# First norm taken on the token rows and transposed a second time; early work of the last delta head put in another order

## What is computed

```python
h = rmsnorm(x, norm_w[0])                       # 320 x 2048
proj = h @ delta_w_in                           # q, k, v, z and 64 gate columns
... causal convolution, gated delta rule over 32 value heads ...
x = x + out @ delta_w_out                       # 4096 -> 2048
h = rmsnorm(x, norm_w[1])
... causal multi-scale pooling, gate, pool_w_out ...
x = x + out ; y = rmsnorm(x, final_norm_w)
```

## Time and profile before

| | |
|---|---|
| median of three runs | 2074.68 us (2072.94 to 2075.6) |
| the profiled execution, its own time | 2073.34 us |
| its span | 2071.6 us |
| TensorE busy (matmuls) | 2045.4 us, 99% of the span |
| DVE busy | 1261.4 us, 61% |
| ACT busy | 934.5 us, 45% |
| mean granted clock of TensorE | 0.993 |

### The profile page before, as it was taken

How to read it: one execution, slowest core, us unless ns; L and a number is a source line. 1 busy time by engine, 2 the same in 40 slices (tenths; PEclk the granted TensorE clock), 3 DMA queues, 4 the chain that set the end, 5 groups by cost and what they waited for, 6 DMA issues and landing times.

```text
span 2071.6 us, 51668 instructions
## 1 busy us (share of the span) xinstructions
PE 2045.4 (99%) x19451; PEld 1962.3 (95%) x19451; DVE 1261.4 (61%) x2245; ACT 934.5 (45%) x2013; POOL 155.3 (7%) x354
## 2 busy tenths in 40 slices
PE   8999999999999999999999999999999999999997
PEld 7999999999999999999899999999999999999997
DVE  5766677776667777667744445545546656644444
ACT  5555555555555556555533334333333333433333
POOL 4111011100101111010000010000000000000010
PEclk9999999999999999999999999999999999999999
DMA  6544555544455555445544445454454445444442
GB/s 208 163 137 127 162 152 163 152 137 132 138 163 153 153 151 146 123 139 164 162 152 157 140 145 178 143 163 144 152 167 147 150 141 164 158 156 148 143 157 77
DMA packets 381227, 311.13 MB, mean 150 GB/s; under 512 B 20041, under 2 KB 377114, under 8 KB 380570
## 3 DMA queue, kind: packets, MB, share of 16 engines
q1 hardware_dynamic: 379290, 306.30, 48.7%
q10 hardware_dynamic: 1872, 3.96, 0.6%
HBM read 283.85 MB, written 27.25 MB: 150 GB/s over the span
## 4 chain that ended last, share of the span: by engine, by line
PE 92%; DVE 6%; issue 1%; ACT 1%; DMA 0%; POOL 0%; DVEq 0%; ACTq 0%; POOLq 0%; SPq 0%
PE ps L298 27%; PE ps L299 26%; PE ps L300 26%; PE ps L1220 10%; DVE s_s L1153 2%; PE ps L1375 2%; DVE wlo L289 1%; DVE silu L1016 1%; DVE silu L1014 1%; DVE amat L1163 1%; PE ps L1346 0%; DVE xlo L893 0%; DVE xlo L1008 0%; DMA ht<-ht_save 0%; PE ps L1349 0%
## 5 line engine op out<-in xcount | busy, mean ns | idle before, releaser
L298 PE MATMUL ps<-xhi,whi 128*128 128x320 f32 x3072 | 984.8, 321 | 3.9 <-DVE wlo L289 2.6
L300 PE MATMUL ps<-xhi,wlo 128*128 128x320 f32 x3072 | 950.4, 309 | 0.0
L299 PE MATMUL ps<-xlo,whi 128*128 128x320 f32 x3072 | 950.2, 309 | 0.0
L289 DVE TENSOR_TENSOR wlo<-wraw,whi 128x1024 fp32r<-128x1024 f32 (+1 forms) x484 | 582.0, 1223 | 236.6 <-ACT whi L284 234.1
L284 ACT ACTIVATE whi<-wraw 128x1024 fp32r<-128x1024 f32 (+1 forms) x484 | 498.6, 1050 | 309.7 <-PE ps L300 278.6
L298 PEld LDWEIGHTS ps<-xhi,whi 128*128 128x128 f32 x3072 | 578.0, 188 | 28.4 <-issue 13.8
L299 PEld LDWEIGHTS ps<-xlo,whi 128*128 128x128 f32 x3072 | 578.7, 188 | 0.9
L300 PEld LDWEIGHTS ps<-xhi,wlo 128*128 128x128 f32 x3072 | 577.9, 188 | 0.0
L298 PE MATMUL ps<-bhi,whi 128*128 128x320 f32 x512 | 157.6, 308 | 0.0
L299 PE MATMUL ps<-blo,whi 128*128 128x320 f32 x512 | 157.6, 308 | 0.0
L300 PE MATMUL ps<-bhi,wlo 128*128 128x320 f32 x512 | 157.6, 308 | 0.0
(11 more groups left out here) (342 smaller groups left out, 2063.5 us busy)
## 6 DMA issues: line engine op xcount, KB each, us to landing
wraw<-in_delta_w_in_dram SPq DMA_DIRECT2D x384, 256.0 KB, 3.0
wraw<-in_pool_w_in_dram SPq DMA_DIRECT2D x256, 256.0 KB, 3.0
wraw<-in_delta_w_out_dram SPq DMA_DIRECT2D x128, 256.0 KB, 3.3
wraw<-in_pool_w_out_dram SPq DMA_DIRECT2D x128, 256.0 KB, 3.2
s_s<-in_state_delta_dram SPq DMA_DIRECT2D x32, 512.0 KB, 6.1
out_dram<-s_s SPq DMA_DIRECT2D x32, 512.0 KB, 4.2
wraw<-in_pool_w_group_dram SPq DMA_DIRECT2D x64, 256.0 KB, 3.1
dec<-gc_rows SPq DMA_DIRECT2D x16, 320.0 KB, 4.1
```

Of the source, the lines that this page charges most:

```text
L289: nc.vector.tensor_tensor(wlo[:, slot, 0:width], wraw[:, slot, 0:width], whi[:, slot, 0:width].bitcast(F32), ALU.subtract).then_inc(E("w_l ...
L298: mm(o, whi[:, slot, w], hi[:, k_x, :], start=first, stop=False)
L299: mm(o, whi[:, slot, w], lo[:, k_x, :], start=False, stop=False)
L300: done = mm(o, wlo[:, slot, w], hi[:, k_x, :], start=False, stop=last)
```

## The change

At the start, the scale by the reciprocal root is applied to the token rows (`x_rows`, in the memory of `branch`), by ACT for the first block of 128 tokens and by DVE for the other two, in two halves of 1024 channels. PE transposes these rows once more, tile after tile, in the same five banks. The weight goes into the two split operations, which read the transposed tile: ACT's copy to `xhi` takes it as a scale, DVE's to `xlo` is one multiply and subtract. `gates_tile(k - 5)` stands behind the transposes of tile k. The diagonal blocks, `rb`, the ring `sq` and the six matmuls on them go. Copies to `ht` are divided anew between ACT and DVE, DVE's first three stand ahead of the mean, and 24 small matmuls of the warm-up become 4.

In the last head, the quarters 1 to 3 of the branch split and the first two weight splits are spread over the head's first steps, and the two early jobs come two splits later.

```diff
-    BY_ACT = (0, 2, 4, 6) + tuple(range(8, KT))
-    BY_DVE = (1, 3, 5, 7)
+    BY_ACT = (3, 4, 6, 8, 10, 12, 14)
+    BY_DVE = (0, 1, 2, 5, 7, 9, 11, 13, 15)
...
     (ACT, start)
+        tile(3)
+        act.wait_ge(E("rinv"), 1)
+        for h in range(2):
+            c = slice(1024 * h, 1024 * h + 1024)
+            sc.activation(x_rows[:, c], xtok[:, 0, c], ACT.Copy, scale=small[:, 9:10]).then_inc(E("xs_act"), 1)
+        for k in BY_ACT[1:]:
             tile(k)
+        act.wait_ge(E("vecs"), 1)
         for k in range(KT):
+            if k % 4 == 0:
+                split_hi(act, k // 4, k // 4, 512)
+            act.wait_ge(E("xnorm"), k + 1)
+            sc.activation(xhi[:, k, :], tile_bank(k)[:, 0:T], ACT.Copy, scale=vecs[:, k:k + 1]).then_inc(E("x_hi"), 1)
...
     (ACT, delta)
-            begun()
-            split(0)
-            split(1)
+            if not quarter:
+                split(0)
+                split(1)
             decays(n)
             rounds(act, n)
             cached()
...
             last.then_inc(E("squares"), 1)
+            if quarter:
+                quarter(1)
             act.wait_ge(E("qkv_ps"), n * 3)
...
             last.then_inc(E("squares"), 1)
+            if quarter:
+                split(0)
+                quarter(2)
             act.wait_ge(E("z_evac"), n)
             sc.activation(gate[:], zraw[:], ACT.Tanh, scale=0.5).then_inc(E("z_tanh"), 1)
+            if quarter:
+                split(1)
+                quarter(3)
             split(2)
...
     (DVE, start)
-        tile(1)
+        for k in BY_DVE[0:3]:
+            tile(k)
         dve.wait_ge(E("sumsq"), 3)
...
+        for h in range(2):
+            for m, rows in ((1, P), (2, 64)):
+                v.tensor_scalar(x_rows[0:rows, DM * m + 1024 * h:DM * m + 1024 * h + 1024], xtok[0:rows, m, 1024 * h:1024 * h + 1024],
+                                small[0:rows, 9 + m:10 + m], None, ALU.mult).then_inc(E("xs_dve"), 1)
+        dve.wait_ge(E("vec_ps"), 1)
...
+        for k in BY_DVE[3:]:
+            tile(k)
...
+        for k in range(KT):
+            if k % 4 == 0:
+                split_lo(dve, k // 4, k // 4, 512)
             dve.wait_ge(E("x_hi"), k + 1)
+            v.scalar_tensor_tensor(xlo[:, k, :], tile_bank(k)[:, 0:T], vecs[:, k:k + 1], xhi[:, k, :].bitcast(F32),
+                                   ALU.mult, ALU.subtract).then_inc(E("x_lo"), 1)
...
     (DVE, early jobs)
-            if j in (3, 7):
-                early_job(j // 4)
+            if j in (5, 9):
+                early_job(j // 4 - 1)
...
     (PE, start)
-        for _ in range(24):
+        for _ in range(4):
             one(ps[0:BL, 3, 0:16], ident[0:BL, 0:BL], ident[0:BL, 0:16])
...
         for k in range(KT):
+            if k % 8 == 0:
+                pe.wait_ge(E("xs_act"), k // 8 + 1)
+                pe.wait_ge(E("xs_dve"), k // 4 + 2)
+            if k < 5:
+                tile_kept(pe, max(j for j in range(KT) if j % 5 == k))
+            else:
+                pe.wait_ge(E("x_lo"), k - 4)
+            b = tile_bank(k)
+            tr(b[:, 0:P], x_rows[:, P * k:P * k + P], ident[:])
+            tr(b[:, P:2 * P], x_rows[:, DM + P * k:DM + P * k + P], ident[:])
+            tr(b[:, 2 * P:T], x_rows[0:64, 2 * DM + P * k:2 * DM + P * k + P], ident[0:64, 0:64]).then_inc(E("xnorm"), 1)
+            if k >= 5:
+                gates_tile(k - 5)
+        for k in range(KT - 5, KT):
             gates_tile(k)
-        pe.wait_ge(E("rb"), 1)
+        pe.wait_ge(E("vecs"), 1)
```

More of the change, by code:

```diff
@@ L151, in build @@
     xtok = place(g, "xtok", [3, DM])
[L152 to L155, removed]
+    x_rows = branch[:, 0:20, :].rearrange("p k t -> p (k t)")
     vrow = place(g, "vrow", [P])
@@ L584, in delta_act @@
             act.wait_ge(E(f"x_in{m}"), 16)
-            sc.activation(sq_x[0:rows, DM * m:DM * m + DM], xtok[0:rows, m, :], ACT.Square,
+            sc.activation(x_rows[0:rows, DM * m:DM * m + DM], xtok[0:rows, m, :], ACT.Square,
                           accum_out=small[0:rows, 3 + m:4 + m]).then_inc(E("sumsq"), 1)
-        tile(0)
         act.wait_ge(E("ms"), 1)
@@ L712, in branch_hi, with delta @@
             sc.activation(xhi[:, 4 * ch:4 * ch + 4, :], branch[:, 4 * ch:4 * ch + 4, :], ACT.Copy).then_inc(E("b_hi"), 1)
-        def delta(n, split, cached, store, next_silus, begun, v_next, tail_next):
-            begun()
-            split(0)
-            split(1)
+        def delta(n, split, cached, store, next_silus, quarter, v_next, tail_next):
+            if not quarter:
+                split(0)
+                split(1)
             decays(n)
@@ L841, in out_split @@
             split_hi(act, OUT_A + LEAD + j, (LEAD + j) % 4)
-        def out_begun():
-            for ch in range(1, 4):
-                branch_hi(ch)
         act.wait_ge(E("w_used"), OUT_A)
         branch_hi(0)
-        delta(NH, out_split, lambda: None, lambda: None, lambda: None, out_begun, lambda: None, lambda: None)
+        delta(NH, out_split, lambda: None, lambda: None, lambda: None, branch_hi, lambda: None, lambda: None)
     def delta_dve(dve):
@@ L1017, in silus, with delta @@
                                    ).then_inc(E("silu"), 1)
[L1019 to L1023, removed]
+        def delta(n, d, split, conv_next, weights_next, decays_next, silus_next, quarter):
+            if not quarter:
+                split(0)
+                split(1)
             rounds(dve, n)
@@ L1252, in delta_pe @@
                     last = tr(ps[:, 2, P * h:P * h + P], crow[:, h, :], ident[:])
-            if k == 6:
-                pe.wait_ge(E("consts"), 8)
-                pe.wait_ge(E("diag"), 1)
-                for m, rows in enumerate((P, P, 64)):
-                    last = one(ps[:, 0, P * m:P * m + rows], ones[0:rows, :], diag[0:rows, P * m:P * m + rows])
-                last.then_inc(E("rb_ps"), 1)
-        for k in range(KT):
+                last.then_inc(E("vec_ps"), 1)
+        for k in range(KT):
+            if k % 8 == 0:
[12 more added lines that the diff above has]
+        for k in range(KT - 5, KT):
             gates_tile(k)
-        pe.wait_ge(E("rb"), 1)
+        pe.wait_ge(E("vecs"), 1)
         def project(i, at, count):
```

49 lines of the change are left out of this document (5 added, 44 removed).

## The result

| | before | after |
|---|---|---|
| median of eight runs each | 2073.57 us (2071.18 to 2075.6) | 2080.74 us (2079.39 to 2083.98) |
| the profiled execution, its own time | 2073.34 us | 2079.39 us |
| its span | 2071.6 us | 2077.7 us |
| TensorE busy | 2045.4 us | 2055.3 us |
| mean granted clock | 0.993 | 0.990 |

The ratio is 1.0038, interval 1.0028 to 1.0047: slower by 7.2 us. The forecast was 2068.9, the range ended at 2074.0.

A forecast was written before the change was run, and what follows sets the result against it. PE, busy for 99% of the span, was taken as the bound, so only its waits and low-clock stretches could be won. 2073.34 - 5.4 (last head) - 0.3 (start) = 2067.6 profiled, median 1.3 above: 2068.9; range 2065.6 to 2074.0.

The forecast's parts named there:

- What it takes: Start, second round of transposes with gate tiles: PE sets the pace, 17.3 us in sum, ending at 39.3.
- rival 4: Start: clock stays low through the whole second round, costing 6.9 us, 9.1 more if transposes double; 2075.8 to 2084.9; chance 0.09.
- the row of 12 to 22 us: Start: PE did almost nothing but transposes at clock 1.00, cited against the clock staying low in the second round.
- Rival 3: Start: the short warm-up's idle 2 us lowers the clock before the transposes; 2070.6 to 2072.3 us; chance 0.17.
- Rival 2: Start: second transposes are cheaper than 0.57 us a tile, -3 us at the start, 2066.2 us; chance 0.10.
- Begin of the second round: Start: after the scaling by ACT and DVE and the tile copies, the second round begins at 22.0 us.
- Waits of the start: Ahead of the first projection matmul: PE's 1.07 us wait for DVE's low part of the weight goes.
- The last head: Last head: waits -4.0, clock -5.1, a new wait +2.0, clock loss behind it +1.7; sum -5.4 us.
- the new wait: Last head: PE waits 2.0 us for DVE's third quarter, until 1011.8 us.
- a low stretch: Last head, behind the wait on the third quarter: a clock loss of 1.7 us, bounds 0 and 3.4.
- rival 1: Last head: the clock stays full after the wait on the third quarter, 1.7 us less, 2067.2 us; chance 0.22.
- rival 5: Last head: another wait stands right behind those removed, so only 2 us are gained, 2072.4 us; chance 0.04.

The follow-up runs named there:

- s_bridge: `start_alone` with 24 instead of 4 small warm-up matmuls and three unread matmuls between the two rounds of transposes: 2082.87 us, ratio 1.0035 to the kernel before.
- head_alone: The kernel before with only the change's new last head: 2070.12 us against 2074.40, ratio 0.9981.
- s_hold: `start_alone` with 27, not 20, large warm-up matmuls, unread ones behind first-round tiles and five second-round tiles, three between rounds: 2078.39 us, ratio 1.0021 to kernel before.
- b_warm4: The kernel before with only the warm-up edit, 4 small matmuls instead of 24: 2162.32 us, ratio 1.0399.
- start_alone: The kernel before with only the change's new start: 2086.05 us, ratio 1.0058.
- s_plain: `start_alone` with the second round's transposes written as plain matmuls by the identity: 2088.82 us, ratio 1.0076 to the kernel before.

## Why the prediction was wrong

**The step that failed** is the forecast's term "What it takes": 17.3 us for the second round, priced at the full clock. It measured 50.05 - 22.02 = 28.0, at a clock of 0.50 from 22.2 to 49.5 us. Tiles took 0.91 in place of 0.57, steps 1.82 in place of 1.11, gate tiles by themselves 0.80 in place of 0.44. With the clock full the same round took 17.0 (`s_bridge`), so the prices were right for that clock. That the clock would stay low was rival 4, given a chance of 0.09.

Two arguments led there. The first was the row of 12 to 22 us, transposes at 1.00, read as proof that transposes hold the clock. It shows only that it had not fallen yet: with one and the same first round it fell at 12.6, 13.0, 18.0, 19.3 or 22.2 us in other profiles. The second was the pricing of the low stretch that the kernel before has in this stage. It was read rightly as hidden by DVE, and then dropped; but the change takes DVE's second operation away, so the cover goes with it. The prediction had the row, 10 us at the low clock, and should have asked what it costs once PE sets the pace.

**The size.** The projection began 50.05 - 39.3 = 10.75 us later than forecast, nearly all of the 11.8 between 2067.6 and 2079.39. Rival 4's price, 6.9 to 16 us, holds that, but not by its parts. The 0.87 us of a gate tile "at the low clock" is DVE's pace in that stretch: DVE's tiles came 0.87 apart at the low clock (30.00 to 30.87) and 0.86 at the full one (35.80 to 36.66). The low clock alone makes it 0.80. And a tile of transposes did not double, it took 0.34 more. From these, 16 x (0.36 + 0.34) = 11.2. Rival 3's cause, the short warm-up, was part of it: the idle time ahead of x is one place where the clock fell. But the full warm-up with the bridge of `s_bridge` kept the clock up only in part of the executions. Rival 2 is out: at the full clock the second transposes took 0.57 a tile, as the first.

**Begin of the second round.** Forecast 22.0, measured 22.02. DVE's timeline has the four scales:

```profile
14.45 2.73 DVE L871 TENSOR_SCALAR branch<-xtok,small 128x1024 f32<-128x1024 f32 x4
```

Starts tell 2.65 us for four, 0.66 each (the next operation begins at 17.10), for 0.79 forecast; the 2.4 us estimated from "VectorE: DVE Perf Modes", section "The perf-mode tier table", in the Trainium skill was the nearer. That the begin agrees to 0.02 us is partly luck. PE waited 0.20 us for DVE's copy of tile 5 and began tile 10 at 17.85, 0.25 earlier than forecast; the handing over from PE to DVE and back at tile 15, put at nothing, took 0.26 (21.27 to 21.38 and 21.87 to 22.02).

**Waits of the start.** The 1.07 us on `wlo` went, as forecast.

**The last head.** Forecast -5.4, measured -5.0, and -4.3 between medians for the head alone. The waits on `pc` and for the second early job went (4.0); the new wait was 1.94 us for 2.0 forecast, at 1022 since the head comes 10 us late, and a low stretch of 3.4 us followed, 1.7 us of full-speed work, as priced. In the profile of `head_alone` none followed the same wait, and the head itself gained 6.5, against 7.1 by rival 1: that rival held in this one execution. No further wait stood behind those removed: rival 5 is out.

**What stays open.** What exactly the chip wants from PE to grant the full clock is not settled: transposes by themselves raised the clock at the end of every kernel and did not in the second round, and 10.6 us of plain matmuls by themselves did not either. Shown is only that the light first round with its gaps lets the clock fall at a moment that differs between profiles, that the mixed part keeps a full clock full (`s_bridge`, `s_hold`), and that it did not raise a low one in the 18 us that it lasts in the changed kernel (27.3 to 45.5). And why 40 instruction records fewer cost `b_warm4` its 22 waits, while `start_alone`, which has fewer too, is spared, was not followed further.

## What to carry to other kernels

Ask of each stretch at a low clock who paces it: where another engine does, it is nearly free (with 6.8 to 10.2 us of it DVE's stretch at the start took 19.7 to 20.0 us), and a change that relieves that engine makes PE pay for it in full. A window at the full clock doesn't show that its instructions hold it; compare executions, and count light matmuls (transposes, short ones) behind a gap as a risk of half the clock: at this start it came back only with gate tiles by themselves, or with other matmuls beside the transposes or in their place. When two edits come together, time them apart: here the head alone, better ordered, is worth 7.2 us, and the start took more than that away.

## What was not expected of the hardware

- Transposes and nothing else, 2.8 us of them, brought the granted clock from 0.50 back to 1.00 at the end of the kernel before; in the second round of the changed kernel 18 us of transposes and gate tiles did not.
- Twenty short matmuls fewer (40 instruction records) ahead of a long program made it 88 us slower: 139 instead of 41 instruction packets, and 22 waits on "issue" with up to 3.5 us each. The same matmuls put back at another place brought nearly all of it back (2074.98 us against 2074.13).
- Plain matmuls of 128 columns, back to back for 10.6 us, left a low granted clock at 0.50 (`s_plain`).
- The mean clock of one kernel differs between executions by what amounts to 17 us: `s_bridge` took 2069.29 us at 0.998 and 2086.32 at 0.988.
